# Router logits from rows without the norm's root, two storage areas exchanged, and four conditioning chunks placed in the second block

## The chip, the cores and the metric

The kernel runs on one core of a Trainium2 chip. The metric is the time of one execution on the device, in microseconds (us). Times inside an execution are counted from its first instruction.

## What is computed

Two transformer blocks run over 256 tokens of 1024 channels, all in float32. Block one mixes a pooling branch and a latent attention with 8 heads, adds the result to x, and then applies a mixture of 32 experts. What matters here is the way into the experts:

```python
x = x + mix @ w_out
h = rmsnorm(x, g_ffn_norm)                      # x * rsqrt(mean(x*x) + eps) * g
logits = h @ w_router + b_router                # 256 x 32
top_vals, top_idx = top_k(logits, 4); gates = softmax(top_vals)
# per expert: act = f(h @ w_gate_up[e] + b), y += gate * (act @ w_down[e] + b)
```

Every expert's weights (8 MB and 4 MB) are read from HBM once. Block two is conditioned: `c_2 @ w_ada_2 + b_ada_2` gives six vectors of 1024 (shift, scale and gate for the attention half, and the same for the feed-forward half). Then follow a projection to 3342 columns, 16 heads of three kinds of attention, an output projection whose rows are scaled by the gate vector, a gated feed-forward of 2816, and two more norms.

## The kernel before

Every engine has its program written out by hand. TensorE (`block.tensor`), ScalarE (`block.scalar`), VectorE (`block.vector`), GpSimd and the queue SP (`block.sync`), which issues nearly all loads, meet at semaphores only. Within an engine the order is that of the text. A `wait_ge` holds up everything behind it on that engine.

**Weights.** Outside the experts, weights pass in numbered chunks of up to 1 MB through a ring of 12 slots in SBUF. TensorE (or, for w_down_2, it too) raises the semaphore `chunk_used` after the last product of a chunk, in the order of the numbers. SP issues the loads in the order of the numbers as well, and waits before each until the chunk 12 numbers earlier has been used:

```python
def used_before(n):                    # L154
    return n - SLOTS + 1               # SLOTS = 12, chunk_used counts from 1
sp.wait_ge(chunk_used, used_before(n)) # in load(n), L494
```

The numbers are laid out at L102 to L122: conditioning chunks 0 and 1, the first projection, four more conditioning chunks among the attention's weights, w_out (N_OUT1, N_OUT1B), six conditioning chunks, N_MOE. After the experts: N_AFTER, 8 conditioning chunks; N_IN2, the 14 chunks of w_in_2; N_OUT2, the 4 chunks of w_out_2; 4 conditioning chunks; N_GU2 and N_DN2, the feed-forward. The function `ada(i)` (L641) does the product of the i-th of the 24 conditioning chunks, four matmuls of 512 columns on 32 columns of the array each. `keep_ada` (L1866, VectorE) adds the bias once a segment of chunks is done, and `turn_mod` and `keep_mod` (L873, L1995) turn the result into columns.

**Expert weights** pass in pairs of 2 MB, six for an expert: four of w_gate_up, two of w_down. Nine pair areas exist, the ring (six) and three `third` areas that lie on `qk`, on `xc` and on the end of `store`. The loop over experts (L1001) on TensorE is: gate/up products (L955), the scatter of the expert before (L989), the selection's transpose (L962), the gather of the next expert's rows (L940), the activation's transpose (L967), the down products (L981). VectorE computes a list of overfull experts (L2087 to L2100) while expert 0's gate/up products run, and only then enters its own loop.

**The way into the experts.** `square_sums` (L751) takes sums of squares over channels as 8 products with a column of ones. The last w_out products end, VectorE adds them to x in four parts (L1943, `add_part`), ScalarE squares each part (L1482), VectorE computes the reciprocal root in 12 small steps (L1985, L1728 to L1733), makes two diagonal matrices of it (L1989) and the scaled rows (L1991). TensorE transposes and scales x in one (L885, `turn_scaled`), both engines copy the columns with the gain (`keep_cols`), the router's products follow (L918, then L924), then the bias (L2017), the top four (L2022), ranks (L930 to L934), the selection (L2051), the gather (L940) and expert 0.

**In block two** the projection's chunks c = 0 to 13 are `in2(c, t)` (L1075). After c = 5, VectorE runs `head_norms(0)`, then `scale_weights(N_OUT2)`, which waits for the landing of the first w_out_2 chunk and multiplies it by the gate vector (L2187), and after it the gates' biases (L2199 to L2202, `ff_ready`). `log_sigmoid` (L1562, ScalarE) waits for `ff_ready`, and ScalarE's `keep_soft(0)` (L1574) comes after it. TensorE waits for that with `heads_cols` after in2(6, 0). Further on, `scale_weights` of the other three w_out_2 chunks stands ahead of `decay`'s sums (L2210, `cum_kept`) and of `bias_rows` (L2228), for which TensorE waits in `turn_bias` and `turn_conv` (L1121, L1128).

Of the kernel before, what the change touches and what calls it, by code (L numbers as in the profile page):

```python
# [12 lines left out]
BF16 = mybir.dt.bfloat16  # L13
# [22 lines left out]
WINDOWS = (2, 4, 8, 16)  # L36
Q_LORA, KV_LORA, ROPE, NOPE, VDIM, HEADS = 256, 128, 32, 64, 64, 8
# [49 lines left out]
def in2_ready(lo, hi):  # L87
# [12 lines left out]
ADA_SEGMENTS = (0, 6, 8, 12, 16, 20, 24)  # L100
ADA_BANK = (7, 1, 2, 0, 1, 5)
# [5 lines left out]
N_MOE = N_OUT1B + 2 + 6  # L107
# [6 lines left out]
N_OUT2 = N_IN2 + len(IN2_CHUNKS)  # L114
# [7 lines left out]
          *range(N_AFTER, N_IN2), *range(N_OUT2 + 4, N_GU2)]  # L122
ADA_OF = dict(zip(ADA_AT, ADA_CHUNKS))

# [17 lines left out]
for _h in range(HALVES):  # L142
    for _p in range(HALF_E // 2):
        if _h % TURN < 2:
            _count[half_slot(_h, _p)] += 1
            HALF_LANDINGS[_h, _p] = 16 * _count[half_slot(_h, _p)]
        else:
            HALF_LANDINGS[_h, _p] = 16 * (_h // TURN + 1 + (_p == 1))
# [42 lines left out]
SIGNALS = """x0_in x1_in third0_in third1_in third2_in x_spread const_in const2_in band_in vec_in vec2_in wpool_in bias14_in gfin_in bada_in bgu_in bdown_in router_in  # L191
brouter_in vec_turned vec_cols vec2_turned vec2_cols c_ready rows_ready rows_turned cols_dve cols_act proj_kept
lat_rows lat_turned lat_cols qkv_kept trig_arg trig_ready q_roped k_roped qk_turned q_cols k_cols
diff_done diff_kept mixed_done pooled_kept pool_sq pool_sum pool_cols ada_kept mod_turned mod_cols
# [30 lines left out]
def two_blocks(nc, ins, consts, band, out):  # L225
    with ExitStack() as ctx:
# [83 lines left out]
        ang, turns = (rope_area[:, a:a + NT * HALF].rearrange("p (t n) -> p t n", t=NT) for a in (0, NT * HALF))  # L310
        att_sq = rows[:, 0, :].rearrange("p (f t) -> p f t", f=4)

        sel_g = work[:, 0:128].rearrange("p (t s) -> p t s", t=NT)
        sel_s = work[:, 128:384].rearrange("p (t s) -> p t s", t=NT)
        sel_t = work[:, 384:640]
        xg = work[:, 640:1152].rearrange("p (k s) -> p k s", k=KD)
        g_min, act_buf, sg, act_t, yb = (work[:, a:a + 512] for a in range(1152, 1152 + 5 * 512, 512))
        u_clip = work[:, 3712:4224]
        sel_b = work[0:96, 4224:4256].bitcast(BF16)
        sel_d = work[0:96, 4256:4288].bitcast(BF16)  # L320
        lg = work[:, 4288:4360].rearrange("p (t e) -> p t e", t=NT)
        lr = work[:, 4360:4432].rearrange("p (t e) -> p t e", t=NT)
        top = work[:, 4432:4448].rearrange("p (t e) -> p t e", t=NT)
        logit_parts = work[:, 4736:4736 + T]
        chosen = work[:, 4448:4512].rearrange("p (t e) -> p t e", t=NT)
        gexp = work[:, 4512:4576].rearrange("p (t e) -> p t e", t=NT)
        small = work[:, 4576:4704]
        lr_row, list_f = work[0:1, 4992:5088], work[0:1, 5088:5136]
        list_eq, list_w = (pt[0:1, i, :].rearrange("p (j i) -> p j i", j=4) for i in range(2))
        diag = work[:, 5136:5392].rearrange("p (t n) -> p t n", t=NT)  # L330
        third = [qk[:, :, :].rearrange("p a b -> p (a b)"), xc[:, :], store[:, WORK + 2 * D - 2 * SLOT:WORK + 2 * D]]
# [57 lines left out]
        def chunk_source(n):  # L389
# [17 lines left out]
            if n_ < N_OUT2:  # L407
                a, w = IN2_CHUNKS[n_ - N_IN2]
                return ins["w_in_2"][0][:, a:a + w].rearrange("(k p) n -> p k n", p=P), KD, w
# [51 lines left out]
        def attention_heads(block_no):  # L461

            if block_no == 1:
                for h in range(HEADS):
                    yield (h, qk[0:QK, h, :], qk[0:QK, 8 + h, :],
# [24 lines left out]
        def _(sp):  # L490
# [17 lines left out]
            load_small(cst[:, 0:CONST_FIRST], consts[:, 0:CONST_FIRST], "const_in")  # L508
            for name in VEC_FIRST[:2]:
                load_vec(name)  # L510
            for n in range(SLOTS):
# [12 lines left out]
                if n == 8:  # L524
                    for j in range(4):
                        load_small(mod[32 * j:32 * j + 32, 0:2, :],
# [1943 lines left out]
```

## Time and profile before

| | us |
|---|---|
| three runs, median (lowest, highest) | 1465.42 (1463.99, 1467.93) |
| the profiled execution | 1465.46 |
| its span, first to last instruction | 1463.6 |
| TensorE busy | 1409.3 (96%) |
| VectorE, ScalarE, GpSimd busy | 410.1, 225.0, 21.9 |
| moved by DMA | 497.05 MB, 340 GB/s on average |
| start of the expert loop's products (L955) | 136.19 |
| last scatter of the loop (L989) begins | 1049.09 |

The busy sums say little by themselves: TensorE counts as busy while it works through a product whose weights arrive slowly. The chain of waits and the order of time tell more. Rows of a timeline give start (us), duration (us), engine, line, operation, output and inputs, and in brackets how long the engine idled before and what ended that.

### The profile page before, as it was taken

The page shows a single profiled execution, that of the slowest core. Times are in us where ns is not written, and L with a number is a line of the kernel's source. Part 1 is how long each engine was busy: PE and PEld are TensorE (multiplying, and loading weights), DVE is VectorE, ACT ScalarE, POOL GpSimd, SP SyncE. Part 2 cuts the span into 40 slices and gives each one's busy share as a digit, 9 for nine tenths or more (in the row PEclk, how much of TensorE's full clock was granted, in tenths as well). Part 3 has the DMA queues.
Part 4 walks back from the last instruction along what each step waited for, and adds up shares of the span by engine and source line. Part 5 has one row for each costly group of instructions (what it writes and reads, how often), then busy time and mean ns, then how long its engine had stood idle before and what let it go on. Part 6 is the DMA issues. An engine that isn't in the chain of part 4 may idle for free.

```text
span 1463.6 us, 17945 instructions
## 1 busy us (share of the span) xinstructions
PE 1409.3 (96%) x7194; PEld 753.7 (51%) x7194; DVE 410.1 (28%) x1021; ACT 225.0 (15%) x425; POOL 21.9 (1%) x14
## 2 busy tenths in 40 slices
PE   6998999999999999999999999999899998999999
PEld 5654444444444444344334433443388864888843
DVE  5546311211211111121112111211325563001784
ACT  1332111111111111011101110111123442100000
POOL 3200000000000000000000000000000000000000
PEclk9999999999999999999999999999999999999999
DMA  9978999999999999999999999999994326444400
GB/s 340 354 294 345 413 428 428 428 429 429 428 429 428 429 429 429 428 428 429 429 429 428 428 429 429 429 428 429 415 362 169 115 87 201 141 147 145 160 12 29
DMA packets 83777, 497.05 MB, mean 340 GB/s; under 512 B 6285, under 2 KB 47962, under 8 KB 56762
## 3 DMA queue, kind: packets, MB, share of 16 engines
q1 hardware_dynamic: 83132, 495.46, 83.4%
q10 hardware_dynamic: 606, 1.06, 0.2%
q8 instruction: 26, 0.43, 0.1%
q14 instruction: 13, 0.11, 0.0%
HBM read 495.44 MB, written 1.05 MB: 339 GB/s over the span
## 4 chain that ended last, share of the span: by engine, by line
PE 74%; DMA 21%; DVE 2%; ACT 1%; issue 1%; SPq 0%; DVEq 0%; ACTq 0%
PE PS L955 19%; DMA ring<-in_w_gate_up_dram 13%; PE PS L981 11%; PE PS L1329 11%; DMA qk<-in_w_gate_up_dram 8%; PE PS L940 6%; PE PS L1084 6%; PE PS L1339 5%; PE PS L989 3%; PE PS L773 2%; PE PS L670 2%; PE PS L1208 2%; PE PS L967 1%; PE PS L949 1%; PE PS L962 1%
## 5 line engine op out<-in xcount | busy, mean ns | idle before, releaser
L955 PE MATMUL PS<-ring,store 128*64 128x512 f32 x1360 | 301.0, 594 | 14.0 <-DMA ring<-in_w_gate_up_dram 13.7
L955 PEld LDWEIGHTS PS<-ring,store 128*64 128x64 f32 x1360 | 94.4, 137 | 207.9 <-issue 170.7
L2073 DVE TENSOR_SCALAR store<-PS 128x512 f32<-128x512 f32 x32 | 22.1, 691 | 619.7 <-PE PS L955 619.7
L1329 PE MATMUL PS<-xc,ring 128*128 128x256 f32 x704 | 155.3, 384 | 2.3 <-DVE xc L1769 2.3
L981 PE MATMUL PS<-ring,store 128*64 128x512 f32 x704 | 154.8, 592 | 0.0
L1329 PEld LDWEIGHTS PS<-xc,ring 128*128 128x128 f32 x704 | 135.8, 193 | 21.9 <-DVE xc L1769 2.5
L940 PE MATMUL PS<-store,rows 128*128 128x64 f32 x1056 | 125.2, 272 | 1.3 <-DVE store L2051 1.3
L940 PEld LDWEIGHTS PS<-store,rows 128*128 128x128 f32 x1056 | 123.4, 192 | 2.1 <-issue 2.1
L981 PEld LDWEIGHTS PS<-ring,store 128*64 128x64 f32 x704 | 49.3, 137 | 90.7 <-issue 89.1
L1084 PE MATMUL PS<-ring,xc 128*128 128x240 f32 (+1 forms) x448 | 93.6, 366 | 0.0
L1499 ACT ACTIVATE store<-store 128x512 f32<-128x512 f32 x32 | 20.1, 629 | 452.5 <-DVE store L2073 452.5
L1084 PEld LDWEIGHTS PS<-ring,xc 128*128 128x128 f32 x448 | 83.7, 190 | 6.1 <-issue 1.3
L955 PE MATMUL PS<-qk,store 128*64 128x512 f32 x336 | 75.9, 593 | 6.2 <-DMA qk<-in_w_gate_up_dram 6.2
L989 PE MATMUL PS<-store 64*128 64x512 f32 x264 | 65.6, 615 | 0.7 <-ACT store L1505 0.7
L1505 ACT COPY store<-PS 128x512 f32<-128x512 f32 x32 | 18.7, 585 | 239.1 <-PE PS L981 239.1
L2068 DVE TENSOR_TENSOR store<-PS,vcol 128x512 f32<-128x512 f32 x33 | 22.8, 691 | 108.3 <-PE PS L940 108.3
L955 PEld LDWEIGHTS PS<-qk,store 128*64 128x64 f32 x336 | 23.1, 136 | 51.9 <-issue 39.3
L989 PEld LDWEIGHTS PS<-store 64*128 64x128 f32 x264 | 22.7, 186 | 43.1 <-issue 41.5
L2343 DVE TENSOR_TENSOR store<-store,PS 128x512 f32<-128x512 f32 x11 | 7.6, 687 | 120.4 <-PE PS L1329 120.4
L1499 ACT ACT_TABLE_LOAD x32 | 41.1, 1283 | 0.6
L955 PE MATMUL PS<-store 128*64 128x512 f32 x176 | 39.9, 596 | 0.2
L955 PE MATMUL PS<-xc,store 128*64 128x512 f32 x176 | 39.6, 592 | 0.0
(367 smaller groups left out, 1219.3 us busy)
## 6 DMA issues: line engine op xcount, KB each, us to landing
ring<-in_w_gate_up_dram SPq DMA_DIRECT2D x85, 2048.0 KB, 35.0
ring<-in_w_down_dram SPq DMA_DIRECT2D x44, 2048.0 KB, 37.3
qk<-in_w_gate_up_dram SPq DMA_DIRECT2D x21, 2048.0 KB, 37.5
ring<-in_w_ada_dram SPq DMA_DIRECT2D x24, 1024.0 KB, 15.3
store<-in_w_gate_up_dram SPq DMA_DIRECT2D x11, 2048.0 KB, 34.9
ring<-in_w_gate_up_dram SPq DMA_DIRECT2D x22, 1024.0 KB, 5.1
xc<-in_w_down_dram SPq DMA_DIRECT2D x10, 2048.0 KB, 36.5
store<-in_w_down_dram SPq DMA_DIRECT2D x10, 2048.0 KB, 37.8
```

What stands on the lines that cost most here:

```text
L670: mm = pe.matmul(bank(b)[:, t * w:(t + 1) * w], cols[:, k, t * P:(t + 1) * P], chunk(n)[:, k, :], start=(k == 0), stop=(k == KD - 1))
L773: return pe.matmul(bank(b + 2 * t + h), cols[:, k, t * P:(t + 1) * P], chunk(n)[:, k % 2, h * 512:(h + 1) * 512], start=(k == first), stop ...
L940: mm = pe.matmul(bank(2)[:, k * CAP:(k + 1) * CAP], rows[:, t, k * P:(k + 1) * P], sel_g[:, t, :], start=(t == 0), stop=(t == NT - 1))
L955: mm = pe.matmul(bank(b)[CAP * h:CAP * (h + 1), :], xg[:, k, :], w[:, b * FE + h * 512:b * FE + (h + 1) * 512], start=False, stop=(k == KD ...
L981: mm = pe.matmul(bank(3)[CAP * h:CAP * (h + 1), :], lhs, w[:, (f % 2) * D + h * 512:(f % 2) * D + (h + 1) * 512], start=False, stop=(f == 7))
L989: mm = pe.matmul(bank(4 + 2 * t + h), sel_t[CAP * h:CAP * (h + 1), t * P:(t + 1) * P], yb[CAP * h:CAP * (h + 1), :], start=False, stop=False)
L1084: mm = pe.matmul(bank(b)[:, t * w:(t + 1) * w], cols[:, k, t * P:(t + 1) * P], chunk(n)[:, k, :], start=(k == 0), stop=(k == KD - 1))
L1208: mm = pe.matmul(bank(4 + 2 * t + h), y_cols(k)[:, t * P:(t + 1) * P], chunk(N_OUT2 + k // 2)[:, k % 2, h * 512:(h + 1) * 512], start=(k = ...
L1329: mm = pe.matmul(bank(4 + 2 * (j % 2) + up)[:, f * T:(f + 1) * T], chunk(n)[:, k, f * P:(f + 1) * P], cols[:, k, :], start=(k == 0), stop= ...
L1339: return pe.matmul(bank(SEVEN_BANK[m]), lhs, rhs, start=(i == 0), stop=(i == FT // 2 - 1))
L1499: return nc.scalar.activation(sg, g_min, ACT.Sigmoid, scale=ALPHA).then_inc(done, 1)
L2068: v.tensor_tensor(xg, bank(2).rearrange("p (k s) -> p k s", k=KD), vcol[:, GFFN_AT:GFFN_AT + KD].unsqueeze(2).to_broadcast([P, KD, CAP]), ...
```

## The change

1. The ring's layout: of the six conditioning chunks ahead of the experts two stay (N_MOE becomes 18 instead of 22), and four (i = 16 to 19) move among the chunks of w_in_2, at N_IN2 + 6, 7, 11 and 12. N_OUT2 rises by four relative to N_IN2.
2. On TensorE, ada(6) and ada(7) come after the logits and after the ranks. ada(16) and ada(17) come after in2(6, 0), ada(18) and ada(19) after in2(8, 1), with turn_mod(2) after pair_scores(1). VectorE's `keep_ada` and `keep_mod` follow them.
3. The router's weights are multiplied by the norm's gain beforehand. x is transposed as it is, part by part as `x_added` arrives; the root multiplies the logits. ScalarE makes the scaled rows.
4. The experts' scratch moves to the end of `store` and the third weight area to its beginning; queries and keys of block one alternate in `qk`, so that half of it is free after four heads. SP's order of the first expert pairs follows from that.
5. Sums of squares: VectorE first adds the four groups (one reduce of 1024 elements), and two products remain of eight. The band product skips columns that are zero. The rows of b_ada_2 are loaded once instead of 32 times each. Small semaphores are merged.

```diff
-ADA_SEGMENTS = (0, 6, 8, 12, 16, 20, 24)
+ADA_SEGMENTS = (0, 6, 8, 16, 18, 20, 24)
-N_MOE = N_OUT1B + 2 + 6
+N_MOE = N_OUT1B + 2 + 2
-N_OUT2 = N_IN2 + len(IN2_CHUNKS)
+N_OUT2 = N_IN2 + len(IN2_CHUNKS) + 4
-          *range(N_AFTER, N_IN2), *range(N_OUT2 + 4, N_GU2)]
+          *range(N_AFTER, N_IN2), N_IN2 + 6, N_IN2 + 7, N_IN2 + 11, N_IN2 + 12, *range(N_OUT2 + 4, N_GU2)]
+def n_in2(c):
+    return N_IN2 + c + (2 if c >= R_GATES else 0) + (2 if c >= 9 else 0)
-        third = [qk[:, :, :].rearrange("p a b -> p (a b)"), xc[:, :], store[:, WORK + 2 * D - 2 * SLOT:WORK + 2 * D]]
+        moe = store[:, 2 * SLOT:WORK + 2 * D]
+        third = [qk[:, :, :].rearrange("p a b -> p (a b)"), xc[:, :], store[:, 0:2 * SLOT]]
...
+            for c in (0, 2, 4):
+                load_pair(c)
+            sp.wait_ge(sig["sq_reduced"], 1)
+            load_third(2, 0, 2 * SLOT)
+            sp.wait_ge(sig["scores_done"], HEADS // 2)
+            load_third(0, 0, SLOT)
             sp.wait_ge(sig["scores_done"], HEADS)
+            load_third(0, SLOT, 2 * SLOT)
+            for c in (6, 8):
+                load_pair(c)
             sp.wait_ge(sig["parts_done"], 1)
             load_third(1, SLOT, 2 * SLOT)
+            load_pair(10)
             sp.wait_ge(sig["x_spread"], 1)
             load_third(1, 0, SLOT)
...
-            def square_sums(squares):
+            def square_sums(n):
+                pe.wait_ge(sig["sq_reduced"], n)
                 for t in range(NT):
-                    for f in range(4):
...
+                    mm = pe.matmul(bank((3, 0)[n - 1])[:, t:t + 1], sq_cols[:, t * P:(t + 1) * P],
+                                   ones[:, 0:1], start=True, stop=True)
...
-            for i in range(6, 10):
-                ada(i)
-            turn_scaled()
-            ada(10)
-            ada(11)
+            for t in range(NT):
+                x_ = ffn_order(x_sb[:, t, :])
+                for h in range(2):
+                    pe.wait_ge(sig["x_added"], 2 * t + h + 1)
+                    for k in range(4 * h, 4 * h + 4):
+                        mm = pe.transpose(bank(k // 2)[:, (k % 2) * T + t * P:][:, 0:P], x_[:, k // 2, k % 2, :], ident)
...
-            turn_mod(0, 3)
-            add_x(7)
...
             moe_gather(sig["gathered"])
-            add_x(5).then_inc(sig["x_spread"], 1)
+            add_x(5)
+            add_x(7).then_inc(sig["x_spread"], 1)
...
                 moe_gate_up(weights(0), lambda mm, k: mm.then_inc(chunk_used, 1))
+                if e == 0:
+                    turn_mod(0, 3)
...
             in2(6, 0)
+            ada(16)
+            ada(17)
             pe.wait_ge(sig["heads_cols"], 1)
             turn_soft(2, 6)
             in2(6, 1)
...
+            pe.wait_ge(sig["ada_kept"], 4)
             pair_scores(0)
             in2(8, 1)
+            ada(18)
+            ada(19)
...
             for j in (1, 2, 3):
                 in2(8 + j, 0)
                 pair_scores(j)
+                if j == 1:
+                    turn_mod(2, 3)
```

On VectorE:

```diff
             r_att = rstd(S_MIX, 512, NT, NT)
+            dve.wait_ge(sig["bias_split"], 2)
+            do.step(v.memset(lg[:, :, EXPERTS:EXPERTS + 4], BIG))
+            do.step(v.memset(rank[:, :, :], -1.0))
+            do.step(v.memset(gates[:, :, :], 0.0))
...
-                do.tell(v.tensor_scalar(diag[:, t, :], ident, r_[:, t:t + 1], None, ALU.mult), "rows_ready")
...
+            for t in range(NT):
+                do.step(v.scalar_tensor_tensor(out=lg[:, t, 0:EXPERTS], in0=bank(5)[:, t * EXPERTS:(t + 1) * EXPERTS],
+                                               scalar=r_[:, t:t + 1], in1=brouter[:, :], op0=ALU.mult, op1=ALU.add))
...
             do.tell(v.tensor_copy(lists[:, 0:33], list_f[:, 0:33]), "lists_ready")
+            keep_mod(0, 3)
+            norm_gain(0, 8, "norm1_g_2")
...
             dve.wait_ge(sig["bcast_kept"], 1)
             scale_weights(N_OUT2)
             dve.wait_ge(sig["proj_kept"], len(IN1_CHUNKS) + R_GATES)
-            dve.wait_ge(sig["bias14_in"], 48)
...
             scale_weights(N_OUT2 + 3)
+            keep_ada(3)
             dve.wait_ge(sig["cumt_turned"], 1)
...
             conv_channel(0)
+            keep_ada(4)
             conv_channel(1)
+            keep_mod(2, 3)
+            do.step(v.tensor_tensor(modc[:, 32:40], modc[:, 32:40], modc[:, 40:48], ALU.add))
+            norm_gain(1, 32, "norm2_g_2")
             pair_probs(1)
```

## Rows read from the trace of the kernel before

**Rows 1.** Chain of waits that ended last (start, us, what), expert loop.

```profile
136.39 13.73 PE PS L955 x64
...
164.22 13.73 PE PS L955 x64
...
582.63 37.49 DMA qk<-in_w_gate_up_dram
...
993.74 37.49 DMA ring<-in_w_gate_up_dram
```

**Rows 2.** Busy time in stretches (header gives the columns), ahead of the experts.

```profile
core 0: us, PE busy (x) PEld busy (x) DVE busy (x) ACT busy (x) POOL busy (x), PEclk, DMA share, GB/s
...
80.00:90.00 10.00, 10.00 (x52) 5.78 (x52) 6.94 (x30) 5.78 (x19) 0.00 (x0) 1.00 0.38 160
```

**Rows 3.** Timeline of all engines, 95 to 141 us.

```profile
104.78 1.84 PE L755 MATMUL PS<-cst,rows 128*128 128x1 f32 x16
...
106.73 0.16 DVE L1968 COPY ms<-PS 128x2 f32<-128x2 f32 x1 [8.88 <-PE PS L755]
...
110.29 3.11 DVE L1943 SCALAR_TENSOR_TENSOR xc<-PS,rs,xc 128x512 f32<-128x512 f32 x4 [1.02 <-PE PS L773]
...
114.32 0.16 DVE L1985 SCALAR_TENSOR_TENSOR rs<-ms 128x2 f32<-128x2 f32 x1 [0.93 <-ACT rows L1482]
...
116.69 0.61 DVE L1989 TENSOR_SCALAR store<-cst,rs 128x128 f32<-128x128 f32 x2
...
125.37 0.22 DVE L2017 TENSOR_TENSOR store<-PS,brouter 128x64 f32<-128x64 f32 x1 [0.24 <-PE PS L924]
...
131.13 3.76 PE L940 MATMUL PS<-store,rows 128*128 128x64 f32 x32 [1.34 <-DVE store L2051]
```

**Rows 4.** The page's costliest groups: a ScalarE copy of 512 elements from PSUM.

```profile
L1505 ACT COPY store<-PS 128x512 f32<-128x512 f32 x32 | 18.7, 585 | 239.1 <-PE PS L981 239.1
```

**Rows 5.** Timeline of SP and of VectorE early in the loop.

```profile
139.85 0.33 SPq L564 DMA_DIRECT2D ring<-in_w_gate_up_dram  x1
...
151.17 0.60 DVE L2058 TENSOR_SCALAR store<-cst,rank,gates 128x128 f32<-128x128 f32 x2 [0.63 <-DVE lists L2100]
```

**Rows 6.** Timeline of VectorE, ScalarE and TensorE in block two.

```profile
1095.66 0.95 DVE L2176 TENSOR_REDUCE ms<-rows 128x12 f32<-128x768 f32 x1 [22.10 <-ACT rows L1572]
...
1103.02 2.29 DVE L2187 TENSOR_TENSOR ring<-ring,store 128x2048 f32<-128x2048 f32 x1 [0.54 <-DMA ring<-in_w_out_dram]
...
1107.74 0.17 DVE L2199 TENSOR_TENSOR store<-store,bias 128x12 f32<-128x12 f32 x1 [2.42 <-ACT store L1595]
...
1111.69 3.01 ACT L1579 ACTIVATE qk<-PS,vcol 128x256 f32<-128x256 f32 x6
...
1112.72 0.66 PE L1110 MATMUL PS<-cst,store 128*128 128x128 f32 x4 [1.61 <-ACT qk L1579]
...
1117.30 0.37 DVE L2212 COPY store<-PS 128x10 f32<-128x10 f32 x2 [2.82 <-PE PS L1118]
...
1127.07 1.04 PE L1135 MATMUL PS<-cst,store 128*128 128x128 f32 x8
...
1134.27 0.55 PE L1170 MATMUL PS<-cst,store 128*128 128x128 f32 x3 [1.05 <-DVE store L1910]
```

**Rows 7.** SP's issues in block two, and the ring's times from issue to landing.

```profile
1107.03 0.37 SPq L496 DMA_DIRECT2D ring<-in_w_out_dram  x1
...
1116.65 0.37 SPq L496 DMA_DIRECT2D ring<-in_w_ada_dram  x1
...
DMA to landing us min/median/max: 4.9/10.3/10.6
```

**Rows 8.** Busy time in a stretch after TensorE had waited; columns as in Rows 2.

```profile
1235.00:1241.00 6.00, 5.45 (x13) 4.40 (x14) 0.69 (x1) 0.46 (x1) 0.00 (x0) 0.50 1.10 349
```

**Rows 9.** Timeline of TensorE: conditioning chunks and the turning of their results.

```profile
1051.97 5.36 PE L652 MATMUL PS<-ring,c_rep 128*32 128x512 f32 x48
...
1071.84 1.04 PE L876 MATMUL PS<-cst,mod 128*128 128x128 f32 x8
```

More of the change, by code:

```diff
@@ L317, in two_blocks @@
[L317 to L328, printed above, removed]
+        moe = store[:, 2 * SLOT:WORK + 2 * D]
+        sel_g = moe[:, 0:128].rearrange("p (t s) -> p t s", t=NT)
+        sel_s = moe[:, 128:384].rearrange("p (t s) -> p t s", t=NT)
+        sel_t = moe[:, 384:640]
+        xg = moe[:, 640:1152].rearrange("p (k s) -> p k s", k=KD)
@@ new lines, in two_blocks @@
+        g_min, act_buf, sg, act_t, yb = (moe[:, a:a + 512] for a in range(1152, 1152 + 5 * 512, 512))
+        u_clip = moe[:, 3712:4224]
+        sel_b = moe[0:96, 4224:4256].bitcast(BF16)
+        sel_d = moe[0:96, 4256:4288].bitcast(BF16)
+        lg = moe[:, 4288:4360].rearrange("p (t e) -> p t e", t=NT)
+        lr = moe[:, 4360:4432].rearrange("p (t e) -> p t e", t=NT)
+        top = moe[:, 4432:4448].rearrange("p (t e) -> p t e", t=NT)
+        logit_parts = moe[:, 4736:4736 + T]
+        chosen = moe[:, 4448:4512].rearrange("p (t e) -> p t e", t=NT)
@@ L825, in _ @@
             turn_probs_1(1)
+            square_sums(1)
             pool_columns(1, 1)
@@ L864, in _ @@
             att_columns(5, 1)
-            pe.wait_ge(sig["att_sq"], 4)
-            square_sums(att_sq)
             att_columns(6, 1)
-            att_columns(7, 0)
+            square_sums(2)
+            att_columns(7, 0, (0,))
+            att_columns(7, 0, (1,))
             att_columns(7, 1, (0,))
@@ L927, in _ @@
             add_x(4)
+            ada(6)
             pe.wait_ge(sig["routed"], 1)
@@ L1062, in _ @@
                 add_zero(4 + 2 * t, 5 + 2 * t).then_inc(sig["moe_done"], 1)
-            for i in range(12, 18):
+            for i in range(8, 14):
                 ada(i)
@@ L1724, in _, with root_steps @@
             do = Steps(dve, dve_own, sig)
+            def root_steps(dst, src, tmp, told=None):
+                for i in range(3):
+                    do.step(v.tensor_tensor(tmp, dst, src, ALU.mult))
+                    do.step(v.scalar_tensor_tensor(out=tmp, in0=tmp, scalar=-0.5, in1=dst, op0=ALU.mult, op1=ALU.mult))
+                    last = v.scalar_tensor_tensor(out=dst, in0=tmp, scalar=1.5, in1=dst, op0=ALU.add, op1=ALU.mult)
+                    if told and i == 2:
+                        do.tell(last, told)
+                    else:
+                        do.step(last)
             def rsqrt(dst, src, tmp):
@@ L1729, in rsqrt @@
                 do.step(v.tensor_scalar(dst.bitcast(I32), dst.bitcast(I32), -1.0, RSQRT_GUESS, ALU.mult, ALU.add))
[L1730 to L1733 removed]
+                root_steps(dst, src, tmp)
             def rsqrt_column(dst, src, tmp):
@@ L1944, in add_part, with reduce_squares @@
                                                op0=ALU.mult, op1=ALU.add), told)
+            def reduce_squares(squares):
+                do.tell(v.tensor_reduce(sq_cols, squares.rearrange("p f t -> p t f"), AX.X, ALU.add), "sq_reduced")
             heads_1 = list(attention_heads(1))
@@ L1982, in _ @@
                     add_part(4, t, h, r_att, "x_added")
+            for b in (0, 1):
+                dve.wait_ge(sig["rows_turned"], 4 + b + 1)
+                do.tell(v.tensor_copy(cols[:, 2 * b:2 * b + 2, :], bank(b).rearrange("p (k t) -> p k t", k=2)), "cols_dve")
+            turned[0] += 1
             dve.wait_ge(sig["x_squared"], 4)
```

234 lines of the change are left out of this document (110 added, 124 removed).

## The prediction

> **What bounds the kernel now.** I read the chain of waits first. The expert loop is most of the span. An expert's gate/up products start every 27.6 us at first, and from expert 16 on each expert waits for its fourth pair of weights, 58.7 us for two experts: from 582.63 to 993.74 lie 14 experts, 29.36 us each [rows 1]. So TensorE sets the pace for about 16 experts and the DMA for the rest. At 27.6 us throughout, the last expert would start 1.73 x 16 = 27.7 us earlier. Ahead of the loop the busy times by stretch show a full TensorE and, at 80 to 90 us, DMA engines at 0.38 [rows 2]: the loads there wait for room, not for bandwidth. From 104 us on TensorE waits in turns with VectorE [rows 3]. In block two TensorE is nearly always busy, with two waits that matter here: 1.61 us for ScalarE ahead of turn_soft(2) and 1.05 us ahead of turn_probs(0) [rows 6].
>
> **Up to the last add.** A square_sums of eight products takes 1.84 us [rows 3]; two should take a quarter, 0.45. The first saves 1.3 on a TensorE that is full from 68.8 to 111.8, so all behind it comes 1.3 earlier. The reduce that VectorE does instead is 1024 elements; 768 took 0.95 [rows 6], so 1.27, and it lies beside products at both places. The second square_sums comes after att_columns(6, 1) now: it would end at 105.8. VectorE's copy and root took from 106.73 to 109.26; they now end 2.5 after the sums, and the three memsets that moved here add 0.46, so the first add starts at 108.9 and not at 110.29. Four adds take 3.11 [rows 3]: the last ends at 112.0 instead of 113.4. The band product has 16 matmuls in place of 8; the shortest fp32 product here costs 1.84 / 8 = 0.23, so 16 of them 3.5 against 3.45 now: nothing, within 0.2 either way.
>
> **From the last add to the gather.** Before: square, root (114.32 to 116.65), diagonal, turn with scaling, columns, router, and the logits' bias at 125.37, which is 12.0 after the last add [rows 3]. Now ScalarE squares the last part (0.87) and copies two banks (0.6 each [rows 4]) until 114.1, TensorE's last two router products end near 114.55, and ScalarE's copy and the two small products bring the logits at 116.0 (copy to bias took 1.4 before). VectorE has copied its two banks by 113.5 and done the root by 115.85, 0.15 ahead of the logits. The root is hidden only just: if it isn't, each further 0.1 counts in full. The top four, ranks and selection take 1.5, 1.3, 0.5 and 0.4, the logits 0.25 more for the second instruction, waits 0.5: the gather starts at 120.45 instead of 131.13 [rows 3]. ScalarE's scaled rows (two of 1024 elements, near 1.1 each) end near 118 and are covered. From the gather to the first gate/up product it was 5.06; add_x(7) comes in between now and costs 0.86, of which keep_x hides 0.1, so 126.25 instead of 136.19: **9.9 earlier**. Ends: 11.4 if TensorE picks up at once everywhere, 7.5 if the ping-pong of four engines costs 0.3 at each of eight steps.
>
> **The expert loop.** Only nine pair areas exist. In both kernels all are full or under way when the loop starts, and the first refill can go out only when TensorE has freed a pair, 3.46 us after the start [rows 5]. From there DMA runs without pause at the same rate to the loop's end. So the loop's end moves with its start, and the 4.2 MB and 0.8 MB that no longer come ahead of it don't count a second time. One loss: VectorE's list work ended at 150.5, just after expert 0's gate/up products, and held back its selection (151.17 [rows 5]). The same list now is followed by keep_mod(0), which waits for a turn_mod behind these products: 0.5 later, and the pair that is freed then is one for which the DMA waits. The loop ends **9.4 earlier**.
>
> **Block two, where the chunks went.** Turn_mod(2) leaves the place at 1071.84, half of 0.87 [rows 9]: 0.44 gained there and lost again later. The ring decides the rest. The load of chunk n waits until chunk n - 12 is used. The issues bear this out: the last w_out chunk went out at 1107.03, after the sixth w_in chunk ended near 1106.9, and the next load at 1116.65, after in2(6, 1) [rows 7]. In the changed numbering N_OUT2 is N_IN2 + 18, so its load waits for chunk N_IN2 + 6, which is ada(16), behind in2(6, 0). Before it was N_IN2 + 14 and waited for the third w_in chunk. VectorE waits for its landing in scale_weights(N_OUT2), and queued behind are the gates' sums (ff_ready), for which log_sigmoid and then keep_soft(0) wait on ScalarE, and TensorE in turn_soft(2). On the old clock, less the 0.44:
> - in2(6, 0) ends 1110.6, ada(16) at 0.89 (5.36 for six [rows 9]) ends 1111.6. Issue to landing of 1 MB on an empty queue took 4.9 [rows 7]: 1116.6. The scaling takes 2.29, four small steps 0.8 [rows 6]: ff_ready at 1119.8, where it was 1108.5. ScalarE needed 3.1 from there to keep_soft and 1.05 more to turn_soft(2): 1123.9 instead of 1112.72. **TensorE waits 11.6 us** where it waited 1.61.
> - in2(6, 1) ends 1127.9; only then goes the third w_out chunk out, lands 1133.0 and is scaled by 1135.4. The decay's sums behind it took from 1117.30 to 1120.03 [rows 6]: cum_kept 1138.1. TensorE has done in2(7) by 1135.1 and waits 3.
> - in2(7, 1) frees the fourth: lands 1140.0, scaled 1142.4, keep_ada(3) 0.7, bias_rows 0.65: 1143.85. turn_conv starts there and not at 1127.07 [rows 6]: **16.8 later**.
> - The clock. After two waits of some 2 us the granted clock was 0.50 for 6 us (1235 to 1241 [rows 8]), that is 1.2 GHz, and returned to 2.4. 11.6 us of waiting should do the same. Six us at half clock cost up to 3, and a fall half as long 1.5. I take 2.1, between them, in in2(6, 1), on which the third load hangs: 18.9. The waits of 3 and 2 us may bring a second one, 0 to 3, I take 1.5: **20.4**.
> - ada(18) and ada(19), 1.8, come ahead of turn_probs(0), where 1.05 was waited [rows 6]: 0.75. ada(16) and ada(17) lie in the long wait. turn_mod(2) again 0.44. keep_ada(4) and keep_mod(2) delay pair_probs(1) by about 1, where turn_probs(2) has over 1 in hand: nothing, 1 if not. **1.2**.
>
> Sum: -9.4 + 20.4 + 1.2 = +12.2. On the profiled execution's 1465.46 (its span and 1.9 around it; the median of the runs is 1465.42) that is **1477.7**. Ends of its own range: -11.4 + 16.8 + 1.2 = +6.6, or 1472, and -7.5 + 19.7 + 3 + 2.2 = +17.4, or 1483.
>
> The Trainium skill, DMA: Bandwidth & Descriptors, "Rules for kernel authors", says to issue a DMA early and wait on its semaphore late. The three w_out loads do the opposite here, as each is issued only after the work that it should hide behind. The same page, "Measured", puts 1 MB at 6.15 us; the row says 4.9 from issue to landing. By the page's figure three loads would add an estimated 3.8 us.
>
> **Rivals.**
> 1. The bytes count. If the DMA could use the time freed ahead of the loop, its bound part would end earlier by the 5 MB as well (11.6, at a pair of 2.1 MB in 29.36 / 6 = 4.89 us [rows 1]), -21 in all: 1465.46 - 21.0 + 21.6 = 1466, no change; with a faster ring yet it would end below. It is one mechanism, room for prefetch at 80 to 110 us, and decides if more than nine pairs could be in hand at the loop's start. For it: DMA is the bound at the loop's end, and 0.38 busy at 80 us. Against: third areas and ring are all that is there. 0.07. [...]
> 2. The wait doesn't bite, since w_out is there before 1107.7, when VectorE needs the gates anyway: -9.4 + 1.2 = 1457.3, faster. Against: the slot is ada(16)'s. For: only that I may have misread the numbering. 0.06.
> 3. The start comes earlier but the loop's end stays (a worse pattern of loads at the start costs it): -2 + 21.6 = 1485, slower still. For: a third area is now filled in two parts, and pair 10 goes out late, at 120, though it isn't needed before 147. 0.07.
> 4. The wait is there without falls of the clock: 16.8 + 1.2 - 9.4 = 1474. It lies within the forecast's own range, which has 0.76 in all; 0.04 is for what I don't see.
>
> **Chances.** A measurement of this kernel can tell about 0.3% (4.4 us) from no change. Faster by more: 0.07 (rival 2). Within: 0.10 (rival 1 and the low end). Slower by more: 0.83. The range for 8 in 10 takes the forecast's own range and reaches to rivals 1 and 3: 1466 to 1485.
>
> **What would show it.** Right: the first L955 product near 126; last scatter near 1040; w_out's first load issued right after ada(16), one VectorE wait of 14 us on w_out_2's landing, TensorE idle some 11.5 us ahead of turn_soft(2), then waits of 3 and 2, and the granted clock at 0.5 after the first. Wrong: a loop that starts at 129 or later (root or ScalarE not hidden), a loop's end that moves by 15 or more (bytes count), w_out landed before ff_ready's inputs.

## The result, and the profile after

The changed kernel takes 1490.4 us (median of four runs, 1487.07 to 1491.03), the kernel before, run beside it, 1466.7. The ratio is 1.016 (95% interval 1.0137 to 1.0182): 23.7 us slower, where 12.2 were forecast. The profiled execution took 1487.07 us, its span is 1485.3 against 1463.6.

Where TensorE waited, after (us in total, times, longest):

```profile
PE PS L963 <- DMA ring<-in_w_gate_up_dram: 13.6, 11, 1.2
...
PE PS L1120 <- ACT qk L1607: 11.6, 1, 11.6
...
PE PS L909 <- issue: 5.1, 1, 5.1
PE PS L1135 <- DVE store L2265: 4.2, 1, 4.2
PE PS L735 <- DVE store L1868: 3.0, 1, 3.0
```

L963 is the gate/up product (L955 before); its waits are the same as before. L1120 and L1135 are turn_soft(2) and turn_bias in block two: the forecast wait and its follower. The other two were not foreseen. L735 turns the heads of the queries (q) ahead of the first scores. L909 is add_zero, the first thing behind the expert loop; "issue" says that the profile shows nothing that released it.

Timelines of VectorE and of TensorE in block two, after (they answer to [rows 6, 7]):

```profile
1117.13 2.29 DVE L2229 TENSOR_TENSOR ring<-ring,store 128x2048 f32<-128x2048 f32 x1 [15.05 <-DMA ring<-in_w_out_dram]
...
1136.58 2.29 DVE L2229 TENSOR_TENSOR ring<-ring,store 128x2048 f32<-128x2048 f32 x1 [12.72 <-DMA ring<-in_w_out_dram]
...
1124.43 1.12 PE L1120 MATMUL PS<-cst,store 128*128 128x128 f32 x4 [11.58 <-ACT qk L1607]
1125.34 5.01 PE L1094 MATMUL PS<-ring,xc 128*128 128x240 f32 x16
...
1141.69 0.40 PE L1135 MATMUL PS<-cst,store 128*48 128x128 f32 x2 [4.19 <-DVE store L2265]
1141.93 5.09 PE L1094 MATMUL PS<-ring,xc 128*128 128x240 f32 x16
1146.86 1.04 PE L1145 MATMUL PS<-cst,store 128*128 128x128 f32 x8
```

The two loads in the chain of waits:

```profile
1112.05 4.96 DMA ring<-in_w_out_dram
...
1130.38 6.11 DMA ring<-in_w_out_dram
```

The first w_out load goes out at 1112.05, when ada(16) is done, the third at 1130.38, when in2(6, 1) is, and VectorE waits for each to land before it can scale the chunk. Behind each TensorE wait the same sixteen products of in2 take 5 us in place of 3.4. The clock fell, as the busy time by stretch shows (columns as in Rows 2):

```profile
1125.00:1131.00 6.00, 6.00 (x26) 5.40 (x25) 0.00 (x0) 1.89 (x4) 0.00 (x0) 0.70 0.00 0
...
1142.00:1147.00 5.00, 5.00 (x19) 4.31 (x19) 3.57 (x4) 0.00 (x0) 0.00 (x0) 0.66 0.00 0
```

First miss. Two terms: the rope is the rotation of q by position, six operations of VectorE; the split takes b_down into three bf16 parts, five operations of GpSimd. Timelines of GpSimd, VectorE and TensorE from 50 us on, after.

```profile
53.95 2.18 POOL L2447 TENSOR_TENSOR store<-store,bdown_b 64x1024 f32<-64x1024 f32 x1
...
52.01 4.41 DVE L1867 TENSOR_TENSOR qk<-store,trig 128x256 f32<-128x256 f32 x4 [5.65 <-ACT store L1426]
56.45 3.40 DVE L1868 TENSOR_TENSOR store<-qk 128x256 f32<-128x256 f32 x2
...
59.90 3.40 PE L735 MATMUL PS<-cst,store 128*96 128x128 f32 x16 [3.00 <-DVE store L1868]
...
70.59 0.49 PE L782 MATMUL PS<-qk 96*128 96x128 f32 x2 [1.34 <-DVE qk L1895]
```

The same, before:

```profile
52.18 1.80 DVE L1831 TENSOR_TENSOR qk<-store,trig 128x256 f32<-128x256 f32 x4 [5.65 <-ACT store L1408]
54.02 0.76 DVE L1832 TENSOR_TENSOR store<-qk 128x256 f32<-128x256 f32 x2
...
56.37 1.48 POOL L2397 CAST bdown_b<-store 96x1024 bf16<-96x1024 f32 x1 [20.11 <-DMA store<-in_b_down_dram]
```

Before, GpSimd's split of b_down began behind VectorE's rope of q. Now b_down lands 3.5 us earlier though it is issued 1.9 us later (42.48 and 40.58). Ahead of it in the queue b_ada's six loads have 4 KB each and not 128, as they are no longer broadcast to all rows. That this is why it lands earlier is read from these sizes; no run put the broadcast back. The split (52.83 to 60.7) now lies on the rope, which takes 7.8 us in place of 2.6. TensorE waits 3.0, the first score product comes at 70.59 and not 65.87, and in between the clock falls:

```profile
60.00:64.00 4.00, 4.00 (x19) 3.74 (x20) 1.29 (x1) 2.33 (x4) 0.74 (x1) 0.57 1.06 439
```

Second miss: TensorE's timeline at the loop's exit, before and then after.

```profile
1049.09 1.99 PE L989 MATMUL PS<-store 64*128 64x512 f32 x8 [0.69 <-ACT store L1505]
1051.01 1.04 PE L902 MATMUL PS<-identb 1*128 1x512 bf16 x4
...
1065.26 6.75 PE L1084 MATMUL PS<-ring,xc 128*128 128x240 f32 x32
```

```profile
1044.65 1.99 PE L997 MATMUL PS<-store 64*128 64x512 f32 x8 [0.69 <-ACT store L1533]
1051.72 1.89 PE L909 MATMUL PS<-identb 1*128 1x512 bf16 x4 [5.08 <-issue]
...
1065.60 6.72 PE L1094 MATMUL PS<-ring,xc 128*128 128x240 f32 x32 [0.48 <-issue]
```

The queue q8, which loads instructions, moves 0.43 MB in 26 packets in the whole run, 16 KB each. I take it for TensorE's, as it moves 27 packets in the kernels with 114 and 142 instructions added to TensorE (below). It moved this between 1046 and 1050 us in the changed kernel; before, between 1048 and 1052, it moved nothing:

```profile
q8 instruction: 1, 0.02, 1.6%
```

The 21.7 us by which the span grew, from these rows: the last scatter starts 4.4 earlier; from there to in2's start it takes 20.95 in place of 16.17, so +4.8; from in2's start to turn_conv 81.26 in place of 61.81, +19.4; from there to the end +1.9.

### The profile page after: what moved, and what is told of

Its sections match the earlier page's. It is cut to its first block, busy times and chain, and to the rows that moved or that the text cites. A ratio compares the mean times of both kernels' runs of the same rounds, so it can differ in the third digit from the quotient of the medians.

```text
span 1485.3 us, 17890 instructions
## 1 busy us (share of the span) xinstructions
PE 1414.5 (95%) x7170; PEld 754.4 (51%) x7170; DVE 418.7 (28%) x1018; ACT 227.1 (15%) x426; POOL 21.7 (1%) x14
## 4 chain that ended last, share of the span: by engine, by line
PE 70%; DMA 21%; DVE 3%; issue 1%; ACT 1%; SPq 0%; DVEq 0%; ACTq 0%
PE PS L963 19%; DMA ring<-in_w_gate_up_dram 13%; PE PS L989 11%; PE PS L1347 10%; DMA qk<-in_w_gate_up_dram 8%; PE PS L1094 6%; PE PS L948 6%; PE PS L1357 4%; PE PS L997 3%; PE PS L1218 2%; PE PS L788 2%; PE PS L975 1%; DMA ring<-in_w_out_dram 1%; PE PS L957 1%; PE PS L970 1%
## 5 line engine op out<-in xcount | busy, mean ns | idle before, releaser
L963 PE MATMUL PS<-ring,store 128*64 128x512 f32 x1360 | 300.8, 594 | 14.1 <-DMA ring<-in_w_gate_up_dram 13.6
L963 PEld LDWEIGHTS PS<-ring,store 128*64 128x64 f32 x1360 | 93.9, 137 | 208.3 <-issue 171.4
L1094 PE MATMUL PS<-ring,xc 128*128 128x240 f32 (+1 forms) x448 | 96.9, 375 | 0.5 <-issue 0.5
L963 PE MATMUL PS<-qk,store 128*64 128x512 f32 x336 | 75.9, 594 | 6.2 <-DMA qk<-in_w_gate_up_dram 6.2
L963 PEld LDWEIGHTS PS<-qk,store 128*64 128x64 f32 x336 | 23.2, 137 | 51.8 <-issue 39.2
L2229 DVE TENSOR_TENSOR ring<-ring,store 128x2048 f32<-128x2048 f32 x15 | 34.4, 2292 | 29.0 <-DMA ring<-in_w_out_dram 28.5
L963 PE MATMUL PS<-store 128*64 128x512 f32 x176 | 39.9, 596 | 0.2
```

What stands on the lines that cost most here:

```text
L963: mm = pe.matmul(bank(b)[CAP * h:CAP * (h + 1), :], xg[:, k, :], w[:, b * FE + h * 512:b * FE + (h + 1) * 512], start=False, stop=(k == KD ...
L1094: mm = pe.matmul(bank(b)[:, t * w:(t + 1) * w], cols[:, k, t * P:(t + 1) * P], chunk(n)[:, k, :], start=(k == 0), stop=(k == KD - 1))
L2229: do.tell(v.tensor_tensor(chunk(n), chunk(n), gate_b[:, :].unsqueeze(1).to_broadcast([P, 2, D]), ALU.mult), "w_scaled")
```

## Experiments

My theories after the comparison: (R) the ring: w_out's late slots make VectorE wait in its queue; (G) GpSimd's split beside the rope; (C) a part of TensorE's program that has to be loaded at the loop's exit. The kernel before ran beside each group of runs, at 1468 to 1469 us. "Less" below counts from the changed kernel's 1490.4, which was measured beside a kernel before at 1466.7, so a gain may be 1 to 3 us larger than it says. Comments in the diffs are mine, and say where a line stands.

**The four scalings of w_out moved behind bias_rows.**

```diff
-            scale_weights(N_OUT2)          # and N_OUT2 + 1, + 2, + 3 from their places
+            for k in range(4):             # behind "bias_rows"
+                scale_weights(N_OUT2 + k)
```

> The changed kernel, with VectorE's four scalings of block two's w_out moved behind bias_rows; rings, loads and TensorE's order stay as they are. Ring theory (the loss in block two is VectorE waiting in its queue for w_out chunks whose slots come free late): TensorE's waits of 11.6 us ahead of turn_soft(2) and 4.2 us ahead of turn_bias, and the slow clock behind them, go; first turn_conv matmul near 1130 us of the trace and not 1147, time near 1473 us (1470 to 1478, the upper part if the 9.2 us of scalings now delay the first row maxima). Rival (the moved conditioning products and the other order on TensorE cost the time themselves): at most 5 us better, 1485 or more.

1472.25 us, 18.1 less (ratio to before 1.0018, 0.9999 to 1.0037). In2's start and turn_conv:

```profile
1071.41 6.72 PE L1094 MATMUL PS<-ring,xc 128*128 128x240 f32 x32 [0.48 <-issue]
...
1132.93 1.04 PE L1145 MATMUL PS<-cst,store 128*128 128x128 f32 x8
```

No wait at L1120 or L1135; in2's start to turn_conv took 61.5 us. TensorE waited 3.4 us further on (L1180) for VectorE's probabilities, which now come behind the scalings. R holds. This profile's turn_conv is at 1132.93 and not 1130, because its whole front part was later.

**Only the first scaling moved behind the gates.**

```diff
-            scale_weights(N_OUT2)          # ahead of the gates' sums
+            scale_weights(N_OUT2)          # behind "ff_ready"
             scale_weights(N_OUT2 + 1)
```

> The changed kernel, with only the first w_out scaling moved behind the gates' ff_ready, just ahead of the second. Ring theory with the loads in a row: the 11.6 us ahead of turn_soft(2) go, but decay_ready waits for the second chunk, cum_kept for the third and bias_rows for the fourth, each issued only when a slot comes free on TensorE: turn_conv near 1137 to 1138 us, 9 to 11 us better, 1479 to 1481 us. Rival (the first load's wait was the whole price): 16 to 19 us better, 1471 to 1474 us.

1484.72 us, 5.7 less (1.0106, 1.0069 to 1.0142): less than either forecast. Timeline of VectorE and TensorE:

```profile
1138.00 2.29 DVE L2229 TENSOR_TENSOR ring<-ring,store 128x2048 f32<-128x2048 f32 x1 [10.25 <-DMA ring<-in_w_out_dram]
...
1122.62 0.57 PE L1126 MATMUL PS<-store,cst 128*128 128x10 f32 x2 [5.78 <-DVE store L2248]
...
1123.89 9.17 PE L1094 MATMUL PS<-ring,xc 128*128 128x240 f32 x32
...
1141.87 1.94 PE L1145 MATMUL PS<-cst,store 128*128 128x128 f32 x8 [5.35 <-DVE store L2270]
```

One wait gone, two others in its place: 5.8 us for the decay and 5.4 for bias_rows, and between them in2(7) in 9.17 us where it takes 6.73 at full clock (the granted clock is 0.71 from 1123 to 1133 us). As in2(7, 1) frees the fourth slot, the slow clock delays the fourth load too: the 9 to 11 us left that fall of the clock out.

**The conditioning chunks behind in2's second chunk.**

```diff
-          N_IN2 + 6, N_IN2 + 7, N_IN2 + 11, N_IN2 + 12,
+          *range(N_IN2 + 2, N_IN2 + 6),
...
-    return N_IN2 + c + (2 if c >= R_GATES else 0) + (2 if c >= 9 else 0)
+    return N_IN2 + c + (4 if c >= 2 else 0)
...
+                    for i in range(16, 20):    # TensorE, behind in2's second chunk
+                        ada(i)
...
-            ada(16)                            # behind in2(6, 0)
-            ada(17)
...
-            ada(18)                            # behind in2(8, 1)
-            ada(19)
```

> The changed kernel, with the four conditioning chunks put behind in2's second chunk instead of behind its sixth and ninth, so that the four w_out loads wait for in2's chunks 2 to 5 again, as before the change; VectorE's order stays. Ring theory: the w_out loads are issued by about 1107 us again, no scaling waits more than 1 us for its chunk, turn_conv near 1130 us plus the two further products, time 1471 to 1475 us. Rival (VectorE's order or its work is the cause, not the ring): no change, 1488 to 1491 us.

1471.86 us (1.0020, 1.0000 to 1.0039), with VectorE's order untouched; L1120 waits 1.6 us, as before the change, and in2's start to turn_conv takes 65.1 us, near 61.8 and the 3.6 of four conditioning chunks. R is shown from both sides: by VectorE's order in the first run, by the ring's in this one.

The profiled execution of this kernel, at 1463.53 us, is the quickest of its eleven, the next being 1469.17. Its rope and the turn of q's heads:

```profile
51.97 1.80 DVE L1865 TENSOR_TENSOR qk<-store,trig 128x256 f32<-128x256 f32 x4 [5.65 <-ACT store L1424]
53.80 3.41 DVE L1866 TENSOR_TENSOR store<-qk 128x256 f32<-128x256 f32 x2
...
57.26 1.95 PE L735 MATMUL PS<-cst,store 128*96 128x128 f32 x16 [0.40 <-DVE store L1866]
```

The split began at 53.44 here, 0.6 us later than in the changed kernel, and met only the last two operations of the rope; TensorE waited 0.4 us and its clock stayed at 1.00. So what the first miss costs hangs on less than a microsecond of timing and can differ between executions of one kernel. The other ten have no trace.

**GpSimd's split held until k_roped.**

```diff
                 pool.wait_ge(sig[loaded], 48)
+                if loaded == "bdown_in":
+                    pool.wait_ge(sig["k_roped"], 1)
```

> The changed kernel, with GpSimd's split of b_down held until VectorE has told k_roped. Contention theory (VectorE's rope of q ran at 1.1 and 1.7 us an operation and not 0.45 and 0.38 because GpSimd's split ran beside it, TensorE waited 3.0 us for it and then ran 4 us at half clock): the rope takes 1.8 + 0.8 us again, no wait ahead of the turn of q's heads, first score product near 65.9 us and not 70.6, first expert product near 126.8 us and not 131.4, time 4.7 us better, 1485.7 us. Rival (the rope was slow for another reason, such as where the tiles lie or the loads): no change in any of these. Third (the start moves but something ahead of the loop, the first weights' landing say, takes it up): rope as in the first, loop start less than 2 us earlier, 1488 to 1490 us.

1484.06 us, 6.3 less (1.0098, 1.0063 to 1.0132). VectorE's timeline:

```profile
55.02 1.80 DVE L1867 TENSOR_TENSOR qk<-store,trig 128x256 f32<-128x256 f32 x4 [5.65 <-ACT store L1426]
56.86 0.76 DVE L1868 TENSOR_TENSOR store<-qk 128x256 f32<-128x256 f32 x2
```

The rope has its old times, TensorE doesn't wait, and the clock stays at 1.00. From the turn of q's heads to the first score product it takes 9.0 us, as before, and 10.7 in the changed kernel. The absolute times missed, as TensorE came to this point 2.9 us later in this execution: over the profiles without added instructions that arrival lies between 56.7 and 61.4 us. What moves it I leave open.

**The contention put into the kernel before.**

```diff
+                    for i in range(3):     # ahead of b_ada's loads and not behind chunk 12
+                        load_small(bdown_f[32 * i:32 * i + 32, :], ins["b_down"][0], "bdown_in")
...
+                if loaded == "bdown_in":
+                    pool.wait_ge(sig["qkv_kept"], 3)
```

> The kernel before, with b_down's load ahead of b_ada's rows and GpSimd's split of it held until the third qkv_kept, which also releases VectorE's rope of q: the two now run side by side in the kernel before as they did by chance in the changed one. Contention theory: the rope's six operations take 6 to 8 us in place of 2.6, TensorE waits 2 to 4 us ahead of the turn of q's heads and then runs some 4 us at half clock, first score product 4 to 6 us later, time 4 to 6 us above the kernel before: 1472.5 to 1474.5 us. Rival (the rope is slow in the changed kernel for its own reasons): rope 2.6 us, time as before within 1 us.

1472.92 us, 3.6 above the median of before (ratio 1.0027, 1.0012 to 1.0042). VectorE, GpSimd and TensorE:

```profile
54.66 5.04 DVE L1830 TENSOR_TENSOR qk<-store,trig 128x256 f32<-128x256 f32 x4 [5.65 <-ACT store L1407]
59.74 3.40 DVE L1831 TENSOR_TENSOR store<-qk 128x256 f32<-128x256 f32 x2
...
54.70 1.29 POOL L2398 CAST bdown_b<-store 96x1024 bf16<-96x1024 f32 x1 [18.08 <-ACT store L1407]
...
63.20 3.65 PE L719 MATMUL PS<-cst,store 128*96 128x128 f32 x16 [3.66 <-DVE store L1831]
```

Here the rope takes 8.4 us, TensorE waits 3.7 for it, and its clock is 0.50 from 63 to 67 us. The rival falls: the rope is slow wherever the split runs beside it. The Trainium skill, SBUF — State Buffer, "SBUF: two separate sides", says of a VectorE operation with two SBUF inputs and a GpSimd operation that reads SBUF that whichever starts first holds the shared ports for the whole instruction. The rows agree: the two last rope operations took 1.7 us each beside GpSimd operations of 1.1 to 2.2, and 0.38 alone.

**24 and then 114 instructions ahead of the loop that do nothing.**

```diff
+            for _ in range(48):            # 228 in the second kernel
+                pe.wait_ge(sig["vec_in"], (len(VEC_FIRST) + 1) * 16)
             ada(0)
```

> The changed kernel with 48 waits that are already met put on TensorE ahead of its first conditioning product: 24 instructions (two waits each) that do nothing but lie ahead of the loop in the program. Code theory (TensorE's 5.08 us of idle ahead of add_zero, which nothing releases, is the loading of the next 16 KB of its instructions: the branch out of the expert loop and over the block for overfull experts lands 331 instructions behind the loop's last one, in a part that was never loaded; before the change the loop ended 114 instructions further on in the program, in the next part of 256, and what lies behind it had been loaded in the loop's first round): 24 instructions are too few to move the loop's end over the border, the idle stays at 4.9 to 5.1 us, time 1490 us. Rival (the idle is a wait for data or for another engine): it stays too, so this run tells only that the added instructions themselves cost under 1 us. Second rival (any shift of the code heals it): idle under 1 us.

> The same with 228 waits: 114 instructions, so that the loop and its exit lie at the same places of TensorE's program as before the change. Code theory: no idle ahead of add_zero (under 0.5 us), the first conditioning product behind the loop follows the last scatter by 2.9 us as before and not by 8.9, time 4 to 5 us better but for what the added instructions cost at the start of the program (0 to 6 us, to be read from the first projection's start): 1485.5 to 1491 us. Rival (a wait for data, another engine or the loads' queue): the idle stays at 5 us.

TensorE at the exit, with 24 (add_zero, the first row of the exit):

```profile
1053.97 1.88 PE L911 MATMUL PS<-identb 1*128 1x512 bf16 x4 [5.14 <-issue]
```

With 114:

```profile
1053.12 1.99 PE L999 MATMUL PS<-store 64*128 64x512 f32 x8 [0.69 <-ACT store L1535]
1055.04 1.04 PE L911 MATMUL PS<-identb 1*128 1x512 bf16 x4
```

C holds: the idle belongs to the place of the code. The times are 1488.09 (one run) and 1488.49 us. The first conditioning product of the 114 waited 12.1 us where it waited 2.3, so the added instructions set it back by 9.8 us and not by the 0 to 6 that I allowed. That hid most of the gain. They lie 0.108 us apart (from 6.7 to 18.8 us). They set VectorE back too: the split of b_down was over at 60.4 us and the rope of q began at 65.3, so this kernel is free of the first miss as well, and its time says little of C alone. The row at the exit does.

**The idle put into the kernel before**, by 142 instructions ahead of TensorE's first wait.

```diff
+            for _ in range(284):
+                pe.wait_ge(sig["go"], 1)   # ScalarE gives it as its first act
```

To make room for "go", "brouter_in" is merged into "router_in" here and in the kernels with 75 instructions below.

> The kernel before, with 142 such instructions ahead of TensorE's first wait: the loop then ends at instruction 2961 and its exit lands at 3292, some 36 to 83 short of a border of 256 by the theory's count, so behind the next one. Code theory: the kernel before now shows the idle of 5 us ahead of its add_zero (L902 of the profile before), which it doesn't have without them; the added instructions take 12 us, about 6 of them beyond the first wait, time near 1468 + 6 + 5 = 1479 us. Rival (the idle belongs to the change's order of work and not to where the code lies): no idle there, 1474 us.

```profile
1073.97 1.88 PE L904 MATMUL PS<-identb 1*128 1x512 bf16 x4 [5.01 <-issue]
```

It is there, in the kernel before. The time, 1487.24 us in one run, is 8 above what I expected: the first wait was 16.2 us and not 12, and a later one of 5.5 came at L672. The 12 came from 9.8 us for 114 instructions, which left out the 2.3 us that TensorE would have waited anyway; at 0.108 us each, 142 take 15.3. The Trainium skill, Runtime: NRT & Kernel Launch, "Instruction fetch mechanics", says that a taken branch out of the loaded window has to wait for the load of its 16 KB. The rows agree, at 4.9 to 5.1 us. Its window of two such parts, of 256 instructions each, they don't bear out: a round of the loop is three experts of about 300 products and weight loads each (904 instructions by my count of the program), and in the changed kernel the queue q8 moved nothing from 275 us to the loop's end.

**Both mends (early chunks, held split), without and with 75 such instructions.** The edits are those above; 75 instructions are 150 waits on "go".

> The changed kernel with both mends: the four conditioning chunks behind in2's second chunk, and GpSimd's split of b_down held until k_roped. If the two losses are independent, their gains add: 1471.9 less 4.7 to 6.3 us (what the mend of the split gave in the trace's account and in its own run) is 1465.6 to 1467.2 us, that is the kernel before within 0.2%, with the 5 us ahead of add_zero still there. Rival (both runs recovered the same thing, or the w_out loads now collide with something else): 1470 to 1473 us.

Without them 1467.89 us (0.9987, 0.9973 to 1.0002), 22.5 less. The two gains alone were 18.5 and 6.3, so they add but for 2.3 us, and the time is 0.7 above the range for it; the rival's 1470 to 1473 is further off. The two losses are separate in the main.

> Both mends (chunks behind in2's second, split of b_down held), and 75 instructions that do nothing (150 waits on a signal that ScalarE gives at its start) put on TensorE ahead of its very first wait, where it is idle for 6.3 to 8.2 us anyway; 114 of them took 9.8 us, so 75 take 6.4 us and are nearly hidden. They move the loop's end to instruction 2780 of the program. Code theory: the idle ahead of add_zero goes (the border lies 36 to 83 instructions ahead of where a count from the program's start has it, since 24 instructions did not cross it), 4.6 us less than the 1467.9 us with both mends alone: 1463 to 1465 us, 0.25 to 0.4% under the kernel before. Rival (75 are not enough, or the added instructions push the start): the idle stays at 5 us, or the first projection starts later by what is gained, 1467 to 1469 us.

With them 1470.18 us (1.0005, 0.9991 to 1.0019): a miss, above the rival's range too. The idle at the exit is gone, and in2 starts at 1060.65. But VectorE and TensorE:

```profile
1108.22 2.29 DVE L2230 TENSOR_TENSOR ring<-ring,store 128x2048 f32<-128x2048 f32 x1 [7.29 <-DMA ring<-in_w_out_dram]
...
1115.52 1.12 PE L1122 MATMUL PS<-cst,store 128*128 128x128 f32 x4 [5.68 <-ACT qk L1608]
```

Here the slots are free in time and the loads are not. Busy time by stretch, of this kernel and of the kernel before:

```profile
1062.00:1095.00 33.00, 33.00 (x175) 27.42 (x174) 4.13 (x16) 4.94 (x8) 0.00 (x0) 1.00 1.07 369
```

```profile
1066.00:1100.00 34.00, 34.00 (x169) 31.06 (x168) 8.22 (x33) 5.10 (x8) 0.00 (x0) 1.00 1.09 364
```

The DMA engines are full at 364 to 369 GB/s in both; with four more 1 MB chunks ahead of w_out, and in2's start 4.6 us sooner than before, w_out is late again.

**The scalings spread, the split held, with and without the 75 instructions**, in the change's own chunk order.

```diff
-            scale_weights(N_OUT2)          # and N_OUT2 + 1, + 2, + 3 from their places
...
+            scale_weights(N_OUT2)          # behind "cum_kept"
...
+            scale_weights(N_OUT2 + 1)      # behind "bias_rows"
+            scale_weights(N_OUT2 + 2)
...
+            scale_weights(N_OUT2 + 3)      # ahead of pair_probs(3)
```

> The changed kernel (its own chunk order) with the four scalings of w_out spread over VectorE's idle stretches (one behind cum_kept, two behind bias_rows, the last ahead of the fourth pair's probabilities), the split of b_down held until k_roped, and the 75 idle instructions ahead of TensorE's first wait. In the run with all three mends of before, the idle of 5 us at the loop's exit was gone, but the first scaling, which stood ahead of the gates, waited 7.3 us for w_out: the loads (365 GB/s for in2's chunks in all kernels, four more conditioning chunks ahead of w_out) had become what bounds block two's first half. Theory: with no w_out chunk wanted before about 1120 us that bound falls away; from in2's start (near 1060.7 us) 61.5 us to turn_conv and 337.7 us to the end give a span of 1460 us, a time of 1461 to 1464 us, 0.3 to 0.5% under the kernel before on this chip. Rival (the loads bound in2 itself, so that TensorE waits for in2's chunks): the 4.6 us come back as waits of in2, 1466 us or more.

> The same without the 75 instructions, so with the idle of 5 us behind the loop: theory 4 to 4.6 us above the run with them, 1465.5 to 1468.5 us. Rival (loads bound this stretch whatever VectorE does): no difference between the two.

1459.99 us with them (0.9942, 0.9925 to 0.9958) and 1465.57 without (0.9975, 0.9962 to 0.9988). The first beats both kernels: 8.5 us under before, 1 us better than its range, and 30 under the change. From the last scatter to in2's start it takes 16.4 us with them and 20.8 without: 4.4 of the 5.6 us between the two, where 4 to 4.6 were expected. What makes the last microsecond stays open. TensorE's way into the loop and its last scatter, without them:

```profile
120.66 3.76 PE L948 MATMUL PS<-store,rows 128*128 128x64 f32 x32 [0.18 <-DVE store L2082]
...
126.58 13.90 PE L963 MATMUL PS<-ring,store 128*64 128x512 f32 x64
...
1039.68 1.99 PE L997 MATMUL PS<-store 64*128 64x512 f32 x8 [0.69 <-ACT store L1533]
```

## Why the prediction was wrong

The direction held and the size didn't: 1477.7 with 1466 to 1485, against 1490.4. The mechanism that the forecast named, the ring, is what it said and cost what it said. Two further losses had no term at all: a start that was taken to be untouched, and the way out of the loop. By its steps:

- **Square sums and adds.** The reduce took 1.93 us and not 1.27, beside other work, as said. From the first score product to the last add's end it was 1.4 less than before, as worked out.
- **Last add to the gather.** The logits' bias follows the last add by 4.25 us (forecast 4.0, before 12.0 [rows 3]), and the root was hidden. With the split held (the last run above), the gather starts at 120.66 (forecast 120.45) and the first product at 126.58 (forecast 126.25). In the changed kernel itself it is 131.44, for a cause that lies 70 us ahead of the gather: the 4.7 us of the rope and its clock. **This is the first step that failed:** "9.9 earlier" took all ahead of the first scores as unchanged, and it was 4.75. I counted b_ada's loads as bytes that don't come twice and never asked what would land sooner without them, or which engine would start on it. The sign that I gave for a wrong forecast, a loop that starts at 129 or later, came true, but not for the reason beside it: root and ScalarE were hidden.
- **The expert loop.** The last scatter moved by 4.4 us where the first product had moved by 4.8, and with the split held by 9.4 (1039.68) where the product had moved by 9.6. So the end follows the start, and the bytes don't count, as forecast; rivals 1 and 3 fall.
- **Behind the loop.** No term in the sum; 4.8 us. **This is the second step that failed,** a stage that the forecast put at nothing. The change took 49 instructions out of TensorE's program in all, by my count, and 114 from ahead of the loop's end; with 114 put back the idle is gone. That alone made the branch out of the loop land in a part not loaded. No row of before showed the price: an estimate was not to be had, but a place for it in the range was.
- **Block two.** TensorE's wait ahead of turn_soft(2): 11.6 forecast, 11.58 measured. VectorE's: 14 and 15.05. Ahead of turn_bias 3 and 4.19; the load of the third chunk took 6.11 us and not 4.9 to 5.1. Ahead of turn_conv 2 and none, since in2(8, 0) at the lower clock covered it. Two falls of the clock, both forecast at 2.1 and 1.5 us; the sixteen products behind each wait took 1.6 and 1.7 us longer. In all 20.4 forecast, 19.4 measured. From turn_conv to the end 1.2 and 1.9. Rivals 2 and 4 fall.
- **Sum.** Forecast -9.4 + 20.4 + 1.2. Measured in the profiles -4.4 + 4.8 + 19.4 + 1.9. The two steps left out are 4.7 and 4.8, together the 9.5 by which the span missed; the small misses of the other terms (0.3, -1.0 and 0.7) cancel, which is luck. The rest of the 23.7 is that the profiled execution was the quickest of the four.

## What to carry to other kernels

When loads are taken away, list what lands earlier and which engine starts on it, GpSimd above all, and lay its operations over VectorE's. A chunk put into a ring moves the issue of every load a ring's length behind it; where an engine scales or casts the landed chunk, keep that step out of the chain that frees the slots. And where a program branches out of a loop, compare the exit's first row before and after: idle with no releaser and a packet on the instruction queue then were the sign here that the code had moved.

## What the runs showed of the hardware

- Taking 16 KB of TensorE's program into reach at a branch costs 4.9 to 5.1 us of idle (nine profiles), with the DMA engines full or nearly. It comes and goes with the place of the code alone; 75 added instructions healed it, 24 did not.
- A satisfied wait is not free on TensorE: instructions that hold two each and do nothing else lie 0.108 us apart, in a row of 114 as in one of 142.
- Six VectorE operations with two SBUF inputs, 2.6 us alone, took 7.8 and 8.4 us beside GpSimd operations of 1.1 to 2.2 us.
- After 3.0 us of TensorE idle the granted clock was 0.57 for 4 us, after 4.2 us 0.66 for 5. After the idle of 5.1 us behind the loop, add_zero's four products took 1.89 us and not 1.04.
